# The causal mask of the diagonal score block: from a TensorE product to a VectorE addition in PSUM

## The reference

```
sc = (q_nope @ k_nope.T + q_rope @ k_rope.T) * ATTN_SCALE      # fp32, 128 x 1024
sc = where(k_pos <= q_pos, sc, -inf)                           # causal
o  = softmax(sc) @ v
```

## Time and profile before

| | |
|---|---|
| three timed runs | 1606.84, 1607.82, 1608.46 us; median 1607.82 |
| profiled execution | 1607.8 us; its span, first to last instruction, is 1607.8 us too |
| TensorE clock granted, mean | 0.997 |
| `project`, 20 to 95 us | PE busy 74.42 of 75 us, DVE 47.96 |
| `attend`, 103 to 484 us | PE busy 375.22 of 381 us, DVE 249.88, ACT 226.71 |
| 484 to 860 us | PE busy 369.97 of 376 us, DVE 216.80 |
| `ffn`, 860 to 1607 us | PE busy 741.00 of 747 us, DVE 409.21 |
| share of DMA engines in `attend` | 0.14 |

### The profile page before, as it was taken

How to read it: one execution, slowest core, us unless ns; L and a number is a source line. 1 busy time by engine, 2 the same in 40 slices (tenths; PEclk the granted TensorE clock), 3 DMA queues, 4 the chain that set the end, 5 groups by cost and what they waited for, 6 DMA issues and landing times. The chain is left out here.

```text
span 1607.8 us, 29621 instructions
## 1 busy us (share of the span) xinstructions
PE 1583.7 (98%) x10341; PEld 1406.4 (87%) x10341; DVE 939.4 (58%) x1818; ACT 587.1 (37%) x1281; POOL 192.1 (12%) x297
## 2 busy tenths in 40 slices
PE   8999999999999999999999999999999999999998
PEld 7988888888886556667889999999999999999996
DVE  5666666666664555546666455544546455455547
ACT  5465565555653333323233131121312213131136
POOL 2000000000001410000003112020211202122000
PEclk9999999999999999999999999999999999999999
DMA  6111111011115765523122020120202111020103
GB/s 227 42 31 30 28 24 25 13 28 26 31 46 168 234 193 163 172 90 95 53 78 80 27 66 21 57 65 26 65 13 65 61 30 53 26 65 14 39 27 119
DMA packets 150583, 109.18 MB, mean 68 GB/s; under 512 B 54623, under 2 KB 139293, under 8 KB 150352
## 3 DMA queue, kind: packets, MB, share of 16 engines
q1 hardware_dynamic: 148272, 100.95, 21.6%
q0 software_dynamic: 1776, 5.71, 1.2%
q10 hardware_dynamic: 432, 1.21, 0.2%
HBM read 101.88 MB, written 10.14 MB: 70 GB/s over the span
## 5 line engine op out<-in xcount | busy, mean ns | idle before, releaser
L1979 PE MATMUL banks<-act_hi,up_hi 128*128 128x352 f32 (+2 forms) x1040 | 335.5, 323 | 0.7 <-PEq L1551 0.7
L1980 PE MATMUL banks<-act_lo,up_hi 128*128 128x352 f32 (+2 forms) x1040 | 335.1, 322 | 0.0
L1981 PE MATMUL banks<-act_hi,up_lo 128*128 128x352 f32 (+2 forms) x1040 | 334.9, 322 | 0.0
L1979 PEld LDWEIGHTS banks<-act_hi,up_hi 128*128 128x128 f32 x1040 | 195.5, 188 | 1.0 <-issue 0.9
L1980 PEld LDWEIGHTS banks<-act_lo,up_hi 128*128 128x128 f32 x1040 | 195.3, 188 | 0.0
L1981 PEld LDWEIGHTS banks<-act_hi,up_lo 128*128 128x128 f32 x1040 | 195.2, 188 | 0.0
L2282 DVE TENSOR_TENSOR o_t<-o_t,banks 128x352 f32<-128x352 f32 x240 | 120.9, 520 | 94.5 <-PE banks L1981 94.2
L2261 DVE SCALAR_TENSOR_TENSOR conv_out<-conv_in,conv_now,conv_out 128x1072 f32<-128x1072 f32 x42 | 63.7, 1517 | 185.6 <-ACT conv_out L2135 185.6
L1056 DVE TENSOR_REDUCE neg_max<-banks 128x1 f32<-128x896 f32 (+7 forms) x128 | 96.6, 755 | 111.3 <-PE banks L828 110.4
L2126 ACT ACTIVATE conv_in<-banks 128x352 f32<-128x352 f32 x84 | 36.3, 458 | 336.2 <-PE banks L1981 336.2
L1979 PE MATMUL banks<-gated_hi,down_hi 128*128 128x352 f32 x480 | 155.8, 325 | 0.0
(11 more groups left out here) (339 smaller groups left out, 3111.2 us busy)
## 6 DMA issues: line engine op xcount, KB each, us to landing
weight_stage<-in_w_f_up SPq DMA_DIRECT2D x44, 512.0 KB, 4.7
c_stage<-in_cache_kv_latent SPq DMA_DIRECT2D x140, 128.0 KB, 2.3
down_stage<-in_w_f_down SPq DMA_DIRECT2D x22, 512.0 KB, 4.2
head_weights_stage<-in_cache_kv_latent SPq DMA_DIRECT2D x56, 128.0 KB, 2.2
rope_query_tab<-in_cache_kv_latent SPq DMA_DIRECT2D x56, 128.0 KB, 2.3
rope_rows<-in_cache_k_rope SPq DMA_DIRECT2D x256, 16.0 KB, 2.0
wo_stage<-in_w_a_out POOLq DMA_DIRECT2D x8, 512.0 KB, 4.5
z<-in_x_prompt SPq DMA_DIRECT2D x8, 512.0 KB, 3.6
```

The costliest lines, as they stand in the source:

```text
L1979: nc.tensor.matmul(o, ws[0], xs[0], start=first, stop=False)
L1980: nc.tensor.matmul(o, ws[0], xs[1], start=False, stop=False)
L1981: return nc.tensor.matmul(o, ws[1], xs[0], start=False, stop=last)
```

## The change

The fourth product of the last score piece goes, and its third product closes the accumulation. DVE's `row_max` gets an addition of the fp32 mask to the last 128 columns of the scores, in place in PSUM, ahead of the reduction, and a semaphore of its own, `dm_ok`, for which the reduction waits. The fp32r copies of mask and identity go, with the staging tile `mask_f`: the DMA writes the mask straight to a tile that lives through `attend`.

```diff
@@ project
-        maskf = sb("mask_f", [P, P])
@@ project, gpsimd
-            pool.dma_start(maskf[:, :], io["mask_diag"]).then_inc(c_in, 16)
+            pool.dma_start(m.mask[:, :], io["mask_diag"]).then_inc(c_in, 16)
@@ project, vector
                     dve.wait_ge(c_in, 80)
-                    nc.vector.tensor_copy(m.maskr[:, :], maskf[:, :])
-                    nc.vector.tensor_copy(m.identr[:, :], m.ident[:, :])
@@ attend
+        dm_ok = s("diag_masked")
@@ attend, tensor, scores
-                    diag = c + wd == (i + 1) * P
-                    last = mm3(o, q, k, True, not diag)
-                    if diag:
-                        last = nc.tensor.matmul(o[:, wd - P:wd], m.identr[:, :], m.maskr[:, :], start=False, stop=True)
+                    last = mm3(o, q, k, True, True)
                 last.then_inc(sc, 1)
@@ attend, vector, row_max
                 src = ps[:, 2 * (n % 2):2 * (n % 2) + 2, :].rearrange("p a c -> p (a c)")[:, 0:wd]
+                nc.vector.tensor_tensor(src[:, wd - P:wd], src[:, wd - P:wd], m.mask[:, :], ALU.add).then_inc(dm_ok, 1)
+                dve.wait_ge(dm_ok, p * NU + n + 1)
                 nc.vector.tensor_reduce(nmax[:, n % 2:n % 2 + 1], src, axis=AXX, op=ALU.max, negate=True).then_inc(nm_ok, 1)
@@ program
-                m.identr, m.maskr = pb("ident_r", [P, P]), pb("mask_r", [P, P])
+                m.mask = pb("mask_diag", [P, P], F32)
```

## The result

The changed kernel takes 1613.47 us (median of 6 runs, 1611.52 to 1614.80) against 1608.18 us before on the same chip (6 runs). The ratio is 1.0032, 95% interval 1.0021 to 1.0044: slower by 5.2 us, between 3.4 and 7.1. Forecast were 1613.9 us and +6.1.

A forecast was written before the change was run, and what follows sets the result against it. PE was taken as full throughout, with DVE lacking room in each head pair's first stretch. Seven pairs (5.8 us) plus the last (0.3) gave +6.1 on 1607.8 us: 1613.9 us, range 1604.0 to 1619.0.

The forecast's parts named there:

- What goes from PE: The 128 mask products: 96 at 0.06 us and 32 at 0.12 us, together 9.6 us of PE.
- rival (1): PE stays the only bound and the additions vanish in DVE's waits: -9.6 us, 1598.2 us; 17%, whole or in part.
- A = 0.33: Delay of each maximum in us: addition 0.29 plus wait for its own result 0.04; ends 0.25 and 0.45.
- rival (3): A dear addition: writing PSUM costs extra or the maximum starts later; 1619.1 us, 14%.
- First place, + 1.05: Units 1 to 5 of a head pair, DVE nearly full: five additions delay PE by 5A - 0.60 = 1.05 us.
- the rival: The experiments' rival: each addition lengthens its unit's way from scores to exp, about 0.116 us anywhere; no chance given.
- Second place, - 0.48: Half-idle DVE window up to unit 13's scores: PE gains six steps of 0.06 and one of 0.12, 0.48 us.
- Third place, + 0.32, and 0.06 back: Units 13 to 15: unit 13's addition delays unit 15's scores through exp by 0.32 us; unit 15's product returns 0.06.
- The boundary: Between head pairs: PE's 0.66 us wait contains no addition, neither absorbs nor adds, so each pair hands its shift on.
- Per pair + 0.83: Sum over one head pair, 6A - 1.15 = +0.83 us; seven such pairs give 5.8 us.
- The last pair, + 0.3: Last head pair, without projections for a next one: the chain through exp at its scores costs +0.3 us.
- Rival (4): Unit 0's additions held up beside POOL's casts by up to 0.4 us: at most 0.1 us a pair, 1614.6; within forecast's 48%.

## Why the prediction was right, step by step

- **What goes from PE.** The price per product held roughly (where a product's time is gained at all, 0.05 to 0.09 us behind a wide block and 0.09 to 0.11 behind a 128-column one, in the kernel without a mask), the conclusion from it only in part: without any mask the attention ends 7.3 us earlier, not 9.6. In the sum of a pair this was allowed for, since only the 0.54 us behind the first stretch were counted. In the price of rival (1) it was not.
- **A = 0.33.** Measured 305.80 to 306.13: 0.33, with 296 ns for the addition. That is 4 ns more than the nearest row, which writes SBUF; the upper end 0.45 and rival (3) fall. So does the cheap end, 0.25.
- **First place, + 1.05.** Measured at unit 7's scores, over the six inner pairs: 1.02 to 1.06 in the changed kernel, 1.02 to 1.10 with the additions of units 1 to 5 alone. That 0.76 us of it are DVE's lack of room is shown by the moved weight split, which gives this much back after the change and nothing before. The other 0.27 are not: with the room made, the scores of units 3 and 5 still start late, held up by exp of units 1 and 3. Unit 1's maximum follows idle time, so there it is the longer chain of its own unit, as the rival has it. "Add nothing" was right only as long as the later wait for the copy was the longer one.
- **Second place, - 0.48.** Measured from unit 7's to unit 13's scores: 1.04 to 0.57, - 0.47. That is six products (units 7 to 12), for which the sum had five times 0.06 and 0.12, 0.42; its seventh step was unit 13's own product, which falls into the next stretch. So the products gave 0.05 us more than priced.
- **Third place, + 0.32, and 0.06 back.** Measured from unit 13's scores to unit 15's: + 0.26, which is A less the 0.06 of unit 13's own product, and 0.07 back behind unit 15. Unit 13 alone shows it: + 0.28 a pair. This is no lack of room, for DVE was idle for 2.25 us ahead of that maximum; it is a chain with nothing to spare.
- **The boundary** hands the shift on: its wait is 0.71 us instead of 0.66, and no more. "PE is full in all three" windows was not quite so: in the third it was busy for 11.79 of 12.10 us.
- **Per pair + 0.83**; over three inner pairs + 0.77, between the first and the last boundary (0.05 to 4.59 us of shift, six pairs) + 0.76. The first pair gave + 0.31 only: unit 7's scores are 0.58 us late in it instead of 1.03, since it loses 0.22 us at unit 2 but nothing at units 3 and 5. It starts behind the projection stage, not behind a boundary; why it differs so stays open.
- **The last pair, + 0.3.** This term was mis-sized: its additions cost 1.19 us. I looked at one link of its chain where there are several. The shift against the kernel before grows by 0.3 at units 3, 5, 9 and 11 and by 0.15 at 14 and at 15. At 3, 14 and 15 the scores start 0.05 us, at 5 0.08 us behind the end of exp of the unit two before. At 9 and 11 exp is done over 1 us earlier, and PE waits for DVE itself ahead of the scores: at 11 the value products wait 0.38 us for DVE's scaling, at 9 a group of transposes takes 0.32 us longer, since its fifth waits for a DVE copy. This group, before and after:

```profile
467.92 0.74 PE L839 MATMUL banks<-ident,probs 128*128 128x128 f32 x5
```

```profile
473.00 1.06 PE L834 MATMUL banks<-ident,probs 128*128 128x128 f32 x5
```

- **Luck in the total.** The seven pairs were put at 5.8 us and gave 0.31 + 6 x 0.76 = 4.9; the last was put at 0.3 and gave 0.80 up to decode. Together 5.7 against 6.1: the two errors cancelled in part, and that the total came so near was in part luck.
- **Rival (1), PE stays the only bound** (with the Trainium skill's rule of the most-contended engine, Trace Analysis, "Identifying the Most-Contended Engine"), fails for the kernel as a whole, which moved the other way. Taken stretch by stretch, as the same page says under "Optimization Strategy" that regimes may differ, it holds in the middle of the inner pairs: there the additions are free and PE's gain is kept.
- **Rival (4)**, the additions beside POOL's casts: no delay shows at the boundary, the additions of unit 0 took 282 to 300 ns and no other unit's less than 285 or more than 300, and a pair with the addition in unit 0 and the middle units comes out within 0.02 us of the sum without it.

## What to carry to other kernels

Don't price work moved between engines by their busy shares over a stage that repeats a pattern: cut one period into windows, find the stretches where the receiving engine has no idle time or where its result is waited for at once, and count only the instructions that land in them, less the idle time that can be used up. Read the first and the last period by themselves: both differed from the inner ones here. Then look at what else that engine does in those stretches: an instruction that nobody waits for yet was worth nothing before this change and the whole net loss after it. And a change need not be made everywhere; with that instruction moved, twelve of the sixteen additions of an inner pair were free or better, and one unit in sixteen carried over a third of the loss.

## What I had not expected of the hardware

A VectorE addition that reads and writes PSUM in place takes 296 ns for 128 x 128, against 292 for the same shape out of PSUM into SBUF. And between two executions the granted clock behind the idle time ahead of decode differed (0.84 and 0.91 over the same 129 products), and these products took 1.6 us less: a third of the effect measured here, and one reason why single profiles of two kernels can't be subtracted at their ends.
